# Prompt and sample cross attention of a decoder step in one block, with the sample heads in four column groups of TensorE

## The reference, cut to what matters

```python
def _cross_attend(h, mk, mv, w_cq, w_co):
    b, t, _ = h.shape
    q = (h @ w_cq).reshape(b, t, CROSS_HEADS, CROSS_HEAD_DIM) * CROSS_HEAD_DIM ** -0.5
    s = jnp.einsum('bthe,bmhe->bhtm', q, mk).astype(jnp.float32)
    p = jax.nn.softmax(s, axis=-1).astype(mv.dtype)
    o = jnp.einsum('bhtm,bmhe->bthe', p, mv).reshape(b, t, D_MODEL)
    return o @ w_co
```

## Time and profile before

| | us |
|---|---|
| median of 3 executions | 4459.39 |
| lowest and highest | 4457.73, 4460.78 |
| span of the profiled execution, first to last instruction | 4467.6 |
| PE busy in it | 3948.9 (88%) |
| DVE, ACT, POOL busy in it | 1918.9, 1238.4, 77.4 |

### The profile page before, as it was taken

One profiled execution on the slowest core, in us unless ns is written; L12 is line 12 of the kernel. 1 busy time (PEld: TensorE's weight loads), 2 busy tenths in 40 slices (PEclk: granted clock), 3 DMA queues, 4 the chain that ended last, 5 costly groups with the idle time before them and its releaser, 6 DMA issues. The chain is left out here.

```text
span 4467.6 us, 73766 instructions
## 1 busy us (share of the span) xinstructions
PE 3948.9 (88%) x30029; PEld 3593.7 (80%) x30029; DVE 1918.9 (43%) x2612; ACT 1238.4 (28%) x1462; POOL 77.4 (2%) x120
## 2 busy tenths in 40 slices
PE   8989986757629998888998879999999999999998
PEld 8989975532228886778998419999999999999997
DVE  3224347758685555433232113333434334343343
ACT  3111126647613333422131202221211212122122
POOL 0000000000000000000000000000000000000000
PEclk9999988879858888999999989999999999999999
DMA  4322237759500000472222352222222222222222
GB/s 151 114 104 85 94 131 245 246 186 375 198 38 1 0 0 15 158 259 99 84 76 103 113 191 94 75 86 95 86 95 95 86 95 86 95 90 91 93 88 77
DMA packets 104474, 501.85 MB, mean 112 GB/s; under 512 B 14305, under 2 KB 20898, under 8 KB 67650
## 3 DMA queue, kind: packets, MB, share of 16 engines
q1 hardware_dynamic: 98082, 479.16, 30.1%
q0 software_dynamic: 6208, 19.93, 1.2%
HBM read 474.55 MB, written 24.50 MB: 112 GB/s over the span
## 5 line engine op out<-in xcount | busy, mean ns | idle before, releaser
L2112 PE MATMUL ps<-hf_hi,whi_f 128*128 128x260 f32 x2816 | 568.3, 283 | 19.1 <-DVE x L2102 11.1
L2112 PE MATMUL ps<-hf_hi,wlo_f 128*128 128x260 f32 x2816 | 567.9, 283 | 0.0
L2112 PE MATMUL ps<-hf_lo,whi_f 128*128 128x260 f32 x2816 | 567.0, 283 | 0.0
L182 ACT ACTIVATE whi_f<-raw 128x2048 fp32r<-128x2048 f32 x132 | 252.8, 1915 | 969.9 <-PE ps L2112 947.6
L2112 PEld LDWEIGHTS ps<-hf_hi,whi_f 128*128 128x128 f32 x2816 | 434.8, 189 | 20.9 <-DVE x L2102 14.5
L2112 PEld LDWEIGHTS ps<-hf_hi,wlo_f 128*128 128x128 f32 x2816 | 434.6, 189 | 0.0
L2112 PEld LDWEIGHTS ps<-hf_lo,whi_f 128*128 128x128 f32 x2816 | 433.6, 188 | 0.0
L186 DVE TENSOR_TENSOR wlo_f<-raw,whi_f 128x2048 fp32r<-128x2048 f32 x132 | 302.6, 2293 | 146.7 <-ACT whi_f L182 146.7
L220 PE MATMUL ps<-h_hi,whi_a 128*128 128x260 f32 x1600 | 324.2, 284 | 29.0 <-DVE h_lo L265 17.7
L220 PE MATMUL ps<-h_hi,wlo_a 128*128 128x260 f32 x1600 | 324.0, 284 | 0.0
L220 PE MATMUL ps<-h_lo,whi_a 128*128 128x260 f32 x1600 | 323.7, 284 | 0.0
(11 more groups left out here) (373 smaller groups left out, 6734.7 us busy)
## 6 DMA issues: line engine op xcount, KB each, us to landing
raw<-w SPq DMA_DIRECT2D x262, 1024.0 KB, 4.8
page_ring<-kc SPq DMA_DIRECT2D x128, 512.0 KB, 4.5
page_ring<-vc SPq DMA_DIRECT2D x64, 512.0 KB, 5.4
page_ring_more<-vc SPq DMA_DIRECT2D x64, 512.0 KB, 5.6
mem_ring<-mkc SPq DMA_DIRECT2D x8, 2048.0 KB, 8.0
mem_ring<-mvc SPq DMA_DIRECT2D x8, 2048.0 KB, 8.1
qkv<-ev_a POOLq DMA_DIRECT2D x24, 260.0 KB, 2.3
qkv_head<-qkv SPq DMA_DIRECT2D x8, 780.0 KB, 6.5
```

The costliest lines, as they stand in the source:

```text
L182: act.activation(whi[:, u, :], raw[:, u, :], ACT.Copy).then_inc(whi_done, 1)
L2112: mm = pe.matmul(ps[:, 2 * u + s, 0:m], wt[:, wslot, kcol:kcol + 128], t[:, k, a:a + m], start=(first and wt is whi and t is th), stop=(la ...
```

## The change

All of it becomes one block. Its lines of code are numbered by the changed kernel here.

- `ring` has four places of 2 MB (`SLOTS`). SP issues, in this order: a quarter of `mkb` (one head), the first sample's keys, the second quarter, the second sample's keys, the third and fourth quarters, `mvb`, and then the samples' other 14 memories, each of them once PE has used its place (`mem_c_used`).
- A sample's matmul has a standing operand of 8 columns for one head, of which only the sample's own column is filled (`qz`, `wz`, set to zero at the start). Head `h` writes partitions `32 h` to `32 h + 7`. All eight samples add into one bank: scores in bank 6, outputs in bank 7, both set to zero at the start. There are still 16 matmuls of 256 columns and 8 of 512 columns a sample. No result goes to HBM and back.
- PE makes a prompt unit's scores two units ahead, and behind them one sample's score matmuls in units 0 to 7, and the value matmuls of one, one, one, one, two and two samples in units 10 to 15. The samples' softmax is done once, on 128 partitions, by DVE and ACT in unit 8, and its transposes by PE in unit 9.
- The prompt's scores use three banks, transposes one (two before), outputs two (four before): PE now waits for ACT's copy of output `e - 2`, and for the copy of the transposes of unit `n - 1`.
- After the last unit ACT copies bank 7, PE transposes it (4 transposes), and DVE puts it in `qc` (4 copies).

The core of the diff, first SP and the new functions on PE:

```diff
+                    def memory(n):
+                        if n >= SLOTS:
+                            sp.wait_ge(mem_c_used, n - SLOTS + 1)
+                        src = (mkc, mvc)[n // NS][n % NS, :, :, :].rearrange("p a b -> p (a b)")
+                        sp.dma_start(ring[:, n % SLOTS, :], src).then_inc(mem_c_in[n % SLOTS], 16)
+                    def sample_scores(b):
+                        pe.wait_ge(mem_c_in[b % SLOTS], 16 * (b // SLOTS + 1))
+                        for e in range(4):
+                            for h in range(XH):
+                                k = 4 * h + e
+                                mm = pe.matmul(ps[32 * h:32 * h + NS, 6, 0:MEM], qz[:, k, b, :], ring[:, b % SLOTS, k * MEM:(k + 1) * MEM],
+                                               start=(b == 0 and e == 0), stop=(b == NS - 1 and e == 3))
+                        mm.then_inc(mem_c_used, 1)
+                    def sample_values(b):
+                        n = NS + b
+                        pe.wait_ge(mem_c_in[n % SLOTS], 16 * (n // SLOTS + 1))
+                        for m in range(2):
+                            for h in range(XH):
+                                at = m * D + h * XD
+                                mm = pe.matmul(ps[32 * h:32 * h + NS, 7, :], wz[:, m, h, b, :], ring[:, n % SLOTS, at:at + XD],
+                                               start=(b == 0 and m == 0), stop=(b == NS - 1 and m == 1))
+                        mm.then_inc(mem_c_used, 1)
```

PE's order in the block:

```diff
-                    pe.wait_ge(mkv_in, 32)
+                    pe.wait_ge(zeroed, 3)
                     scores(0)
+                    scores(1)
+                    pe.wait_ge(S.sem, S.at("qz"))
                     for n, (h, i) in enumerate(units):
-                        if n < 15:
-                            scores(n + 1)
-                        pe.wait_ge(W.sem, W.at(f"w{h}{i}"))
-                        if n >= 2:
-                            pe.wait_ge(A.sem, A.at("t%d%d" % units[n - 2]))
+                        if n < 14:
+                            scores(n + 2)
+                        if n < NS:
+                            sample_scores(n)
+                        elif n == 9:
+                            pe.wait_ge(S.sem, S.at("scale"))
...
+                        elif n >= 10:
+                            if n == 10:
+                                pe.wait_ge(S.sem, S.at("wz"))
+                            for b in ([0], [1], [2], [3], [4, 5], [6, 7])[n - 10]:
+                                sample_values(b)
+                        pe.wait_ge(W.sem, W.at(f"w{n}"))
+                        if n >= 1:
+                            pe.wait_ge(A.sem, A.at(f"t{n - 1}"))
```

More of the change, by code:

```diff
@@ L1734, in decoder_kernel @@
             mvb = sb(st, "mv2", [128, 2, D])
+            SLOTS = 4
+            ring = sb(st, "mem_ring", [128, SLOTS, KT * MEM])
             ex = sb(st, "x_exp", [128, 2, MEM])
@@ L1750, in _ @@
                 def _(sp):
-                    sp.dma_start(mkb[:, :, :], mk_o.rearrange("k p n -> p k n")).then_inc(mkv_in, 16)
-                    sp.dma_start(mvb[:, :, :], mv_o.rearrange("m p n -> p m n")).then_inc(mkv_in, 16)
+                    def memory(n):
[4 more added lines that the diff above has]
+                    for h in range(XH):
+                        hs = slice(4 * h, 4 * h + 4)
+                        sp.dma_start(mkb[:, hs, :], mk_o[hs, :, :].rearrange("k p n -> p k n")).then_inc(mk_in[h], 16)
+                        if h < 2:
+                            memory(h)
+                    sp.dma_start(mvb[:, :, :], mv_o.rearrange("m p n -> p m n")).then_inc(mv_in, 16)
+                    for n in range(2, 2 * NS):
+                        memory(n)
                 @block.tensor
@@ L1757, in scores @@
                         h, i = units[n]
-                        if n >= 2:
-                            pe.wait_ge(A.sem, A.at("e%d%d" % units[n - 2]))
+                        if i == 0:
+                            pe.wait_ge(mk_in[h], 16)
+                        if n >= 3:
+                            pe.wait_ge(A.sem, A.at(f"e{n - 3}"))
                         for e in range(4):
-                            mm = pe.matmul(ps[:, n % 2, 0:MEM], qc[:, 4 * h + e, i * 128:i * 128 + 128], mkb[:, 4 * h + e, :],
+                            mm = pe.matmul(ps[:, n % 3, 0:MEM], qc[:, 4 * h + e, i * 128:i * 128 + 128], mkb[:, 4 * h + e, :],
@@ new lines, in _ @@
+                            dve.wait_ge(P.sem, P.at(f"t{n - 2}"))
+                        did(dve.tensor_scalar(nmx[:, b], mxs[:, b], -XS, None, ALU.mult), f"neg{n}")
+                        if n == 8:
+                            dve.wait_ge(mem_c_used, NS)
+                            step(dve.reduce_max(m1, ps[:, 6, 0:MEM], AX.X), "m1")
+                            step(dve.tensor_scalar(nm, m1, -XS, None, ALU.mult), "nm")
+                        dve.wait_ge(A.sem, A.at(f"e{n}"))
+                        did(dve.reciprocal(ri[:, b], rs[:, b]), f"inv{n}")
@@ new lines, in _ @@
+                        did(dve.tensor_scalar(ex[:, n % 2, :], ex[:, n % 2, :], ri[:, b], None, ALU.mult), f"w{n}")
+                        if n == 8:
+                            dve.wait_ge(S.sem, S.at("exp"))
+                            step(dve.reciprocal(inv, part), "inv")
+                            step(dve.tensor_scalar(se[:, :], se[:, :], inv, None, ALU.mult), "scale")
+                        if n == 9:
+                            dve.wait_ge(S.sem, S.at("wT"))
+                            step(dve.tensor_copy(wz[:, :, :, :, :].rearrange("p m h a b -> p (m h) (a b)")[:, :, ::NS + 1],
+                                                 ps[:, 6, 0:MEM].rearrange("p (g n) -> p g n", n=32)[:, :, 0:NS]), "wz")
```

216 lines of the change are left out of this document (54 added, 162 removed).

## The result

The changed kernel takes 4330.77 us (median of 4 executions, 4327.46 to 4332.2) against 4460.09 us before (median of 4, 4457.73 to 4462.3): ratio 0.971, 95% interval 0.9696 to 0.9724. That is 129.3 us less. The profiled execution has a span of 4330.5 us.

What follows compares the result with a forecast made beforehand. PE, busy 88% of the span, was taken as the bound, with 51.8 us idle in the block. Summed steps cut the block from 248.5 to 119.4 us, saving 129.1: median 4459.4 becomes 4330 us, range 4316 to 4366.

Steps and rivals of the forecast that it cites:

- The price of a column group: Samples' matmuls: four column groups run side by side, four times the rate, sample work 27.5 us instead of 110; chance 0.50.
- one queue: Rival, samples' matmuls: one queue for the array, two at a time; block 138 us, median 4349; chance 0.23.
- two rivals: Samples' matmuls: two at a time (block 138, 4349 us, chance 0.23); no overlap (block 189, 4400 us, chance 0.10).
- Switches: PE going into and out of column-group mode: 0.25 us for each of 14 stretches, 3.5 us.
- the upper end: Largest cost taken for PE going into and out of column-group mode: 5.6 us instead of 3.5.
- Slower: Rival: each change of column group stops the array; 0.2 us one way gives 4438 us; chance 0.04, half of it slower.
- Transposes: PE's transposes between a sample's keys and its scores: 0.44 us a pair, in units of 4.1 us.
- The first load: Block's start: first scores at 5.0 us, from 1.4 for 0.5 MB, 3.1 latency and 0.5 hand-overs.
- Keys 2: Third sample's keys: land at 29.3 us; PE waits 8 us and loses 3 more at 1.2 GHz.
- the rival on the queue: Rival: transfers become the bound at 300 GB/s with four memories in flight; block 142 us, median 4353; chance 0.13.
- The sign of a single stop: Trace sign: PE starts about 5 us into the block and stops once, before keys 2, for some 8 us.
- The last memory: Units 14, 15: last memory issued at 98.4, reaches PE 8.0 us later at 106.4; value 7 loses 1.3 us.

Runs made afterwards that it cites:

- Heads outside: Changed kernel with a sample's two loops exchanged, all four score (two value) matmuls of one head before the next head's: 4351.53 us, ratio 0.9753.
- Pairs: Changed kernel with the samples' score matmuls in pairs, two of each head in turn, then the same again: 4334.5 us, ratio 0.9713.
- two groups: Changed kernel with heads 0 and 2 writing partitions 0 to 7, heads 1 and 3 writing 32 to 39: 4353.49 us, ratio 0.9755.
- one group: Changed kernel with all four heads of a sample writing the same partitions 0 to 7: 4396.34 us, ratio 0.9858.
- The groups alone: Kernel before, separate blocks kept, with only head h writing partitions 32 h to 32 h + 3: 4429.84 us, ratio 0.9927.

## Why the prediction was right

The forecast was 4330 us and the changed kernel takes 4330.8. The steps show how much of that is luck; in us from the start of the block, by the timeline of PE. A step ends where PE's next record starts; the last head's outputs, which have none behind them, end after 16 steps of 0.43 us.

| step | predicted | measured |
|---|---|---|
| first scores | 5.0 | 3.9 |
| keys 2 start | 29.3 | 29.5 |
| scores 5 end | 36.4 | 35.2 |
| first head's outputs end | 46.2 | 44.9 |
| second head's outputs end | 70.0 | 68.3 |
| units 8 and 9 end | 75.3 | 73.0 |
| unit 13 ends | 99.1 | 96.4 |
| value 7 starts | 106.4 | 105.6 |
| last head's outputs end | 116.1 | 116.5 |
| last copy ends | 119.4 | 119.2 |

- **The price of a column group**, the step on which all hung, was right and is shown: one, two and four groups take 7.07, 3.63 and 1.91 us for the same 32 records. The reading of L1391 and L1393, a queue for each part of the array, was right as well, with a limit that it couldn't show (four records). It was a further step than the prediction said, since the operands of L1391 and L1393 lie in different halves of the rows too (64*64 in the earlier trace rows); that it holds for groups that differ in columns alone is shown by *Heads outside* and *Pairs*. The program's own loop order gives each group two records before the next group's turn, so it stays below the limit. With the loops exchanged, the rival *one queue* would have been nearly right in its time (4351.5 against 4349), for another reason. The prices of two rivals were right as well: two groups took a block of 138.3 us (138 summed), one group 185.3 (189).
- **Switches.** 0.25 us for going in and out was assumed. In units 4 to 7 it is 0.2: a sample's first record starts 0.31 us after the last of the prompt's scores, and the transposes 0.33 us after the sample's last four, where a step is 0.216. The 0.2 for one way, on which the upper end and the price of *Slower* rest, was a misreading: L1388's second pair of records starts 0.21 us after its first, not 0.107.
- **Transposes** were priced at 0.44 us, the time until both records end. PE's next work starts 0.27 us after the first. So a unit took 3.9 us and not 4.1, and units 4 to 7 lasted 23.4 us where 23.8 were predicted.
- **The first load** came 1.1 us earlier than summed. If the 0.5 MB took the 1.4 us, 2.5 are left for latency and hand-overs, where 3.1 + 0.5 were taken; no run takes the two apart.
- **Keys 2** were right within 0.2 us, and so was the queue's rate (0.42 MB/us taken; 399 GB/s measured in the window up to 2445.4, 427 to 431 in the next three), which settles the rival on the queue. The lower clock after that wait cost 12% of 15.4 us, 1.8 and not 3.0. The sign of a single stop was not right: PE waited for keys 1 too (0.7 us) and for value 7.
- **The last memory.** The term was mis-sized: 1.3 us lost was predicted, 3.3 us of waiting and 12% of 11.0 us, 1.3, at the lower clock measured. PE came to it 2.8 us earlier than summed, 1.2 us of it by the smaller loss after keys 2. The ring ties the transfer to PE, so its issue came earlier too, at 96.2 us and not 98.4. But it took 9.4 us to land and not 8.0. The memory before it was issued only 3.9 us ahead, and two memories at the 0.42 MB/us and 3.1 us of latency that the prediction took would land at 2530.2 together (an estimate), where PE starts at 2530.4. The rows are SP's last two issues, the last one's time to landing, and PE's records around the wait:

```profile
2517.08 4.26 SPq L1767 DMA_DIRECT2D mem_ring<-mvc  x2
...
mem_ring<-mvc SPq DMA_DIRECT2D x1, 2048.0 KB, 9.4
...
2525.21 1.90 PE L1805 MATMUL ps<-mem_ring,x_sample_weights 128*8 128x512 f32 x16
2530.41 3.22 PE L1805 MATMUL ps<-mem_ring,x_sample_weights 128*8 128x512 f32 x16 [3.30 <-DMA mem_ring<-mvc]
```

  So value 7 started 0.8 us early, and with the lower clock, which had no term, the last outputs end 0.4 us late; the tail took 2.7 us and not 3.3. That all these errors cancel to 0.2 us at the end of the block is luck. Moving value 7 gave 4.4 us of the 4.6.
- **The single block.** What it brings was taken as the sum of four idle stretches and hidden loads; alone it is 64 us (4460.3 to 4396.3), with the groups in it 129.3. The groups alone bring 30.5 us. The two together bring 35 us more than their sum, since each removes what limits after the other: without prompt work between the samples, the faster matmuls wait for loads at the lower clock; without faster matmuls, the block is PE's 178 us of work.
- **The end.** L220 starts 124.6 us after the block's start, where 119.4 + 5.3 were summed. It does so at 2549.4 and not near 2558 because the block began 8.6 us earlier.
- No rival showed. The one on the slower side, a stop at each change of group, would have made the four groups slower than one.

The Trainium skill's rule ("TensorE: Matmul & The Clock Gate", Part 3, the mechanism) that matmuls start strictly in program order is not what these runs show: with heads outside, a sample's 32 records take 20 steps where that order would take 29. The Trainium skill's 2.38x for three column tiles (the same page, "Measured speedup vs the span model"), from which the prediction estimated 3.2x for four, gives less than what is measured here, 3.7x for four (7.07 to 1.91 us).

Left open: why PE's clock stayed low longer in one execution than in another after equal waits (9.40 against 7.13 us for the same outputs). The single execution behind each profile can't tell.

## What to carry to other kernels

Matmuls whose standing operand is narrow can run four at a time if their outputs lie in four column groups; the order of the code has to change the group at least every four records (two f32 matmuls). Place the work of each transfer at the time it lands: after this change the only idle time of PE over 0.5 us between the first scores and the tail was where a memory was late, and moving work to those places gave another 11 us (14 in the block). Two changes that each look small alone (30 and 64 us) can be worth much more together when each is the other's next limit, so test them together too.

## What the runs showed of the hardware that I had not expected

- A column group takes four f32 records, one running and three waiting; a fifth blocks later groups. (Four records are two f32 matmuls; no run tells which of the two is counted.) Shown by 20 steps for 32 records with eight of a head together (4.51 us), and by no loss with four together (1.93 and 1.92 us).
- Four f32 streams of 128 partitions each at full rate: 0.216 us for 256 columns, whether one group runs or four.
- With the groups alone PE worked in bursts of about 3.5 us with waits of 1.4 to 3.9 us between them (busy 26.5 of 45.7 us), and the granted clock was 0.65 in the mean of that stretch, between its two levels. So making PE's work shorter gave back a part of the gain: 3.3 to 3.6 us a sample instead of 1.9.
